# Block products in the output projection of a two-layer trunk, and where their sums are made

## The reference

```python
h = _rmsnorm(x, a_norm); proj = h @ a_w_in          # layer 0: conv, gated recurrence, SiLU gate
x = x + (y * silu(gate)) @ a_w_out                  # x1, 512 tokens by 2048
k, v = split(_rmsnorm(x, kv_norm) @ w_kv)           # 16 heads of 128
q, gate = split(_rmsnorm(x, b_norm) @ b_w_in)       # layer 1
o = stick_breaking_attention(q, k, v)
x = x + (o * silu(gate)) @ b_w_out                  # the output projection: 512 x 2048 by 2048 x 2048
return _rmsnorm(x, final_norm)
```

## Time and profile before

| | us |
|---|---|
| three runs: median, lowest, highest | 1676.51, 1676.43, 1677.09 |
| the profiled execution: its time | 1676.65 |
| the profiled execution: its span, first to last instruction | 1674.9 |
| PE, PEld, DVE, ACT, POOL busy | 1663.1, 1391.3, 1030.8, 818.3, 263.4 |
| one pair of heads in the attention stage (1170.66 to 1245.88) | 75.2 |
| last weight unit of attention issued, start of the score products behind it | 1476.87 |
| these score products issued | 1478.77 |
| last matmul issued | 1667.42 |

### The profile page before, as it was taken

How to read it: one execution, slowest core, us unless ns; L and a number is a source line. 1 busy time by engine, 2 the same in 40 slices (tenths; PEclk the granted TensorE clock), 3 DMA queues, 4 the chain that set the end, 5 groups by cost and what they waited for, 6 DMA issues and landing times.

```text
span 1674.9 us, 24069 instructions
## 1 busy us (share of the span) xinstructions
PE 1663.1 (99%) x7767; PEld 1391.3 (83%) x7767; DVE 1030.8 (62%) x1780; ACT 818.3 (49%) x1627; POOL 263.4 (16%) x251
## 2 busy tenths in 40 slices
PE   9999999999999999999999999999999999999998
PEld 7888888888888888887888888888888888888888
DVE  5788887778775554577655646465555646453333
ACT  7655566665555232355645545444444545432223
POOL 0121211122121222310002111101111111103100
PEclk9999999999999999999999999999999999999999
DMA  5555555665532333256755232323233232323223
GB/s 186 176 181 195 171 171 166 197 196 177 149 101 95 94 96 98 94 171 190 241 172 167 82 98 82 101 79 103 75 106 94 81 95 83 101 76 119 95 95 132
DMA packets 179606, 216.95 MB, mean 130 GB/s; under 512 B 12808, under 2 KB 137944, under 8 KB 179416
## 3 DMA queue, kind: packets, MB, share of 16 engines
q1 hardware_dynamic: 179544, 216.16, 41.3%
HBM read 190.95 MB, written 25.17 MB: 129 GB/s over the span
## 4 chain that ended last, share of the span: by engine, by line
PE 96%; DVE 1%; ACT 1%; SPq 1%; DMA 1%; issue 0%; POOL 0%; POOLq 0%; ACTq 0%; DVEq 0%
PE ps L549 94%; PE ps L731 1%; DMA rows_b<-in_b_norm 0%; PE ps L776 0%; SPq L401 0%; SPq L405 0%; SPq L382 0%; DMA v_stage<-in_w_kv 0%; PE ps L579 0%; DVE v_f L1440 0%; DVE rbuf L1335 0%; POOL y_lo L1652 0%; ACT w_hi L835 0%; PE ps L586 0%; DVE v_f L1432 0%
## 5 line engine op out<-in xcount | busy, mean ns | idle before, releaser
L549 PE MATMUL ps<-x_hi,w_hi 128*128 128x512 f32 x1408 | 551.0, 391 | 0.3 <-DVE x_lo L1232 0.3
L549 PE MATMUL ps<-x_hi,w_lo 128*128 128x512 f32 x1408 | 548.4, 389 | 0.0
L549 PE MATMUL ps<-x_lo,w_hi 128*128 128x512 f32 x1408 | 548.1, 389 | 0.0
L1196 DVE SCALAR_TENSOR_TENSOR w_lo<-stage,cT,w_hi 128x256 fp32r<-128x256 f32 x352 | 199.1, 566 | 328.7 <-ACT w_hi L839 328.1
L837 ACT ACTIVATE w_hi<-stage,cT 128x256 fp32r<-128x256 f32 x352 | 178.5, 507 | 375.5 <-PE ps L549 350.6
L549 PEld LDWEIGHTS ps<-x_hi,w_lo 128*128 128x128 f32 x1408 | 264.3, 188 | 55.2
L549 PEld LDWEIGHTS ps<-x_hi,w_hi 128*128 128x128 f32 x1408 | 264.4, 188 | 54.1 <-DVE x_lo L1232 0.5
L549 PEld LDWEIGHTS ps<-x_lo,w_hi 128*128 128x128 f32 x1408 | 264.5, 188 | 53.4 <-issue 0.2
L1193 DVE TENSOR_TENSOR w_lo<-stage,w_hi 128x512 fp32r<-128x512 f32 x160 | 132.6, 833 | 216.1 <-ACT w_hi L835 216.1
L835 ACT ACTIVATE w_hi<-stage 128x512 fp32r<-128x512 f32 x160 | 99.8, 630 | 251.2 <-PE ps L549 249.2
L839 ACT ACTIVATE w_hi<-stage,cT 128x256 fp32r<-128x256 f32 x352 | 174.4, 496 | 0.0
(11 more groups left out here) (206 smaller groups left out, 2301.5 us busy)
## 6 DMA issues: line engine op xcount, KB each, us to landing
stage<-in_a_w_in SPq DMA_DIRECT2D x160, 256.0 KB, 2.8
stage<-in_b_w_in SPq DMA_DIRECT2D x128, 256.0 KB, 2.8
stage<-in_w_kv SPq DMA_DIRECT2D x95, 256.0 KB, 2.8
stage<-in_a_w_out SPq DMA_DIRECT2D x80, 256.0 KB, 2.6
b_raw<-in_w_kv SPq DMA_DIRECT2D x64, 256.0 KB, 3.9
t_scratch<-b_raw SPq DMA_DIRECT2D x64, 256.0 KB, 3.5
stage<-in_b_w_out SPq DMA_DIRECT2D x64, 256.0 KB, 2.5
stage<-t_scratch SPq DMA_DIRECT2D x45, 256.0 KB, 3.1
```

The lines of the kernel that those rows point to most:

```text
L549: mm = pe.matmul(dst, a, b, start=start and n == 0, stop=stop and n == 2, skip_group_check=not check)
L1196: nc.vector.scalar_tensor_tensor(w_lo[:, slot, 0:256], stage[:, slot, 0:256], cT[:, col:col + 1], f(w_hi[:, slot, 0:256]), ALU.mult, ALU.s ...
```

## The change

**Seven products for eight.** O is seen as blocks: token halves (256) by even and odd heads, A11, A12, A21, A22; W as row tiles even and odd by column halves of 512 in each of two groups of 1024, B11, B12, B21, B22. PE makes p1 = A11 B11, p2 = A12 B21, p6, p7, p5 of block sums on both sides, p4 of A22 and a sum of B, p3 of a sum of A and B22, each over eight pairs of heads: 112 steps of six matmuls of 512 columns (`out_product`), two of them in the place of one unit of before while attention runs. Steps 0 to 55 are the first column group; p2, p4 and p3 come last, in turn. The weight ring has six slots. The first use of p7 and p5 stands ahead of the last of p6 (`out_operand`).

**Weight sums in the attention stage.** For each pair SP loads eight 256 KB blocks of W (`wb_load`, after pieces 14 and 18), DVE makes eight differences and sums (`weight_sum`, behind positions 2, 3, 4, 5, 8, 9, 14 and 15), SP stores them in `wt_scratch` (after pieces 22 and 33). In the output projection SP reads them back as operands.

**Sums of O on DVE.** Behind its gate products DVE makes the low part of A11, then three sums and, at position 31, the fourth (the semaphore `o_lo_ready`) and the low part of the second (`s2o_lo`). They go to `o_scratch` in DRAM (640 KB for a pair) and return to `or_raw`, which lies where x1 lay in SBUF, so the return waits for the end of the last weight unit of attention: seven pairs at step 10, the last at step 24. From there ACT and DVE split them in `or_hi` and `or_lo` inside their steps. POOL does none of this any more.

**x1 by tokens.** In stage 2 PE turns every x1 tile (`turn_x1`, eight calls of eight transposes, the last in the value stage), ACT copies it out, SP stores it; 4 MB come back into `x2` at step 24. The block results are added into `x2` by DVE.

**The end.** C11, C21 and C12 of the last column group become ready with the last three steps, for all four token tiles at once. DVE and ACT then add, square, multiply by the gain, norm, scale, first tiles 2 and 3, then 0 and 1.

The diff, cut to the parts of the output projection; indentation is cut too.

```diff
+OB_AT = {14 + 2 * i: i for i in range(VP)}
+OY_AT = {28 + 3 * i: i for i in range(VP)}
+W_SUM = {2: 0, 3: 1, 4: 2, 5: 3, 8: 4, 9: 5, 14: 6, 15: 7}
...
+def out_operand(q):
+    g, o = divmod(q, NO)
+    late = 2 * VP - 1
+    if late <= o < late + OUT_LAST:
+        return operand(q + 1)
+    if o == late + OUT_LAST:
+        return operand(g * NO + late)
+    return operand(q)
...
+def o_store(p, half):
...
+    sp.wait_ge(o_lo_ready, p * 2 + 3)
+    dst = o_scratch[at(p, 1), :, :].rearrange("n p c -> (n p) c")
+    sp.dma_start(dst, ost[:, half, 0:5, :].rearrange("p a c -> p (a c)")).then_inc(o_out, 16)
...
+def out_load(q):
...
+    if q >= VRING:
+        sp.wait_ge(po_lo, q - VRING + 1)
+    elif slot < RING:
+        sp.wait_ge(lo_ready, U4 - RING + slot + 1)
...
+for q in range(VOPS):
+    if q == 4:
+        sp.wait_ge(wb_out[0], 64 * VP)
+    out_load(q)
+    if q == 7:
+        wb_store(PAIRS - 1, 1)
+    if q == 10:
+        sp.wait_ge(w_used, U4)
+        sp.wait_ge(o_out, 32 + 16 * (PAIRS - 1))
+        for p in range(PAIRS - 1):
+            sp.dma_start(or_raw[:, p, :, :].rearrange("p a c -> p (a c)"),
+                         o_scratch[p]).then_inc(or_in, 16)
+    if q == 20:
+        o_store(PAIRS - 1, 1)
         g_row = final_norm.rearrange("(a n) -> a n", a=1)
+        sp.wait_ge(wb_out[1], 64 * VP)
         sp.dma_start(g_fin[:, :], g_row.to_broadcast([P, D])).then_inc(g_fin_in, 16)
+    if q == 24:
+        sp.wait_ge(s2o_lo, PAIRS)
+        x1_v = x1t_scratch.rearrange("(t p) n -> p t n", p=P)
+        for t in range(TT):
+            sp.dma_start(x2[:, t, :], x1_v[:, t, :]).then_inc(x1t_in, 16)
+        sp.wait_ge(o_out, 32 + 16 * PAIRS)
+        sp.dma_start(or_raw[:, PAIRS - 1, :, :].rearrange("p a c -> p (a c)"),
+                     o_scratch[PAIRS - 1]).then_inc(or_in, 16)
...
+def turn_x1(it, b, wait=None):
...
+    for m in range(2):
+        pe.wait_ge(res_step, it * 8 + (4 * b + m + 3))
+        if wait is not None:
+            pe.wait_ge(x1t_taken, wait)
+        for t in range(TT):
+            mm = pe.transpose(ps[2 + 4 * b + m][:, P * t:P * t + P], x1[:, m, P * t:P * t + P], ident[:, :])
+        mm.then_inc(x1_turned, 1)
...
+def out_product(q):
...
+    if name == "p6":
+        if g == 0:
+            pe.wait_ge(s2o_lo, i + 1)
...
+    if name in ("p7", "p5") and g == 0:
+        pe.wait_ge(ob_lo, i + 1)
+    if name in ("p2", "p4", "p3") and g == 0:
+        pe.wait_ge(oy_lo, i + 1)
...
+            if g:
+                pe.wait_ge(c12o_ready, 2 * g)
...
+            pe.wait_ge(c22o_ready, 2 * g + 2)
+    pe.wait_ge(po_lo, q + 1)
+    hi_w, lo_w = out_weights(q)
+    for t in range(2):
+        if name in O_LEFT:
+            m_hi, m_lo, which = O_LEFT[name]
...
+def out_step(q):
...
+        act.wait_ge(w_used, U4 - RING + q + 1)
+    elif q >= VRING:
+        act.wait_ge(po_used, q - VRING + 1)
+    nc.scalar.activation(out_weights(q)[0], out_staged(q), ACT.Copy).then_inc(po_hi, 1)
+    for at, parts, ready in ((OB_AT, slice(0, 2), ob_hi), (OY_AT, slice(2, 5), oy_hi)):
+        if q in at:
+            i = at[q]
+            act.wait_ge(or_in, 16 * (PAIRS - 1) if i < PAIRS - 1 else 16 * PAIRS)
+            if i >= 4:
+                act.wait_ge(s2o_lo, PAIRS)
...
+    if o == 2 * VP + AHEAD_V - 1:
+        act.wait_ge(po_used, OUT_OPERAND[g, VP - 1, "p6"] + 1)
+        if g == 0:
+            act.wait_ge(s2o_lo, PAIRS)
+        else:
+            act.wait_ge(u_added, 6 * g)
+            act.wait_ge(c12o_ready, 2 * g)
+            act.wait_ge(c21o_ready, 2 * g)
...
+def square(ready, g, t, first, c):
...
+    n = next(squared)
+    if n:
+        act.wait_ge(x2_sq, n)
+    nc.scalar.activation(junk[:, :], x2[:, t, 512 * c:512 * c + 512], ACT.Square,
+                         accum_out=ss5[:, t, c:c + 1]).then_inc(x2_sq, 1)
...
+def finish(n, t):
...
+    act.wait_ge(sqrt_in, 3 + n)
     nc.scalar.activation(small[:, 1, t:t + 1], small[:, 1, t:t + 1], ACT.Sqrt).then_inc(sqrt_out, 1)
-    act.wait_ge(rs_ready, 3 + t)
+    act.wait_ge(rs_ready, 3 + n)
+    act.wait_ge(gained, 4)
     nc.scalar.activation(x2[:, t, 0:D // 2], x2[:, t, 0:D // 2], ACT.Identity,
                          scale=rs_tok[:, t:t + 1]).then_inc(scaled_a, 1)
...
+def out_sums(it, half, pos):
...
+        dve.wait_ge(o_out, p * 16 + 16)
+        nc.vector.tensor_tensor(s1_o, a21, a22, ALU.add).then_inc(so_step, 1)
+        dve.wait_ge(so_step, p * 2 + 1)
+        nc.vector.tensor_tensor(s2_o, s1_o, a11, ALU.subtract).then_inc(s2o_raw, 1)
+        nc.vector.tensor_tensor(s3_o, a21, a11, ALU.subtract).then_inc(so_step, 1)
+    if pos == 31:
+        dve.wait_ge(s2o_raw, p + 1)
+        dve.wait_ge(so_step, p * 2 + 2)
+        dve.wait_ge(ost_copied, p + 1)
+        nc.vector.tensor_tensor(s4_o, s2_o, a12, ALU.subtract).then_inc(o_lo_ready, 1)
+        dve.wait_ge(s2o_hi, p + 1)
+        nc.vector.tensor_tensor(oa_lo[:, 0, one, :], s2_o, f(oa_hi[:, 0, one, :]),
+                                ALU.subtract).then_inc(s2o_lo, 1)
 def take_gate(it, half):
...
+def out_step(q):
...
+    hi_w, lo_w = out_weights(q)
+    dve.wait_ge(po_hi, q + 1)
+    nc.vector.tensor_tensor(lo_w, out_staged(q), f(hi_w), ALU.subtract).then_inc(po_lo, 1)
+    for at, parts, high, ready in ((OB_AT, slice(0, 2), ob_hi, ob_lo), (OY_AT, slice(2, 5), oy_hi, oy_lo)):
+        if q in at:
+            i = at[q]
+            dve.wait_ge(high, i + 1)
+            nc.vector.tensor_tensor(or_lo[:, i, parts, :], or_raw[:, i, parts, :],
+                                    f(or_hi(i)[:, parts, :]), ALU.subtract).then_inc(ready, 1)
+    g, o = divmod(q, NO)
...
+        dve.wait_ge(po_used, OUT_OPERAND[g, VP - 1, "p5"] + 1)
+        for t in (2, 3):
+            dve.wait_ge(p7o_added, 2 * g + t - 1)
+            piece(lambda x: nc.vector.tensor_tensor(x, x, ps[4 + t][:, :], ALU.subtract), g, t, 1,
+                  c22o_ready)
+    if g and o == AHEAD_V - 2:
+        make_c11(g - 1)
+    if g and o == AHEAD_V - 1:
+        make_c21(g - 1)
+    if g and o == AHEAD_V:
+        make_c12(g - 1, 0)
+        make_c12(g - 1, 1)
+    if g and o in GAIN_AT:
+        t, c = GAIN_AT[o]
+        if o == min(GAIN_AT):
+            dve.wait_ge(g_fin_in, 16)
+            dve.wait_ge(x2_sq, 8)
+        x = x2[:, t, 512 * c:512 * c + 512]
+        nc.vector.tensor_tensor(x, x, g_fin[:, 512 * c:512 * c + 512], ALU.mult)
+GAIN_AT = {2 * VP + 12 + 2 * n: (n % 4, n // 4) for n in range(8)}
+def piece(op, g, t, h, ready):
+    c = 1024 * g + 512 * h
+    op(x2[:, t, c:c + 512]).then_inc(ready, 1)
...
+    if g < VG - 1:
+        dve.wait_ge(po_used, OUT_OPERAND[g, VP - 1, "p3"] + 1)
+    else:
+        dve.wait_ge(last_done, t + 1)
+    dve.wait_ge(u_added, 6 * g + t + 5)
+    piece(lambda x: nc.vector.tensor_tensor(x, x, ps[6 + t][:, :], ALU.subtract), g, t, 1, c12o_ready)
...
+def gain(t, c):
+    x = x2[:, t, 512 * c:512 * c + 512]
+    nc.vector.tensor_tensor(x, x, g_fin[:, 512 * c:512 * c + 512], ALU.mult).then_inc(gained, 1)
+dve.wait_ge(x2_sq, 14)
+for t, c in ((2, 3), (3, 3), (2, 2), (3, 2)):
+    gain(t, c)
+def finish(n, t, squared):
     one = slice(t, t + 1)
-    link(nc.vector.tensor_reduce(ss[:, one], ss5[:, t, :], AX.X, ALU.add))
-    rsqrt(ss[:, one], small[:, 0, one], small[:, 1, one], small[:, 2, one], rs_tok[:, one], 3 + t,
-          lambda: take(ps[t], t, D - 256, 256))
-    dve.wait_ge(x2_taken, 4 * TT + t + 1)
-    nc.vector.tensor_scalar(x2[:, t, D // 2:D], x2[:, t, D // 2:D], rs_tok[:, one], None,
+    dve.wait_ge(x2_sq, squared)
+    link(nc.vector.tensor_reduce(ss[:, one], ss5[:, t, 0:4], AX.X, ALU.add))
+    rsqrt(ss[:, one], small[:, 0, one], small[:, 1, one], small[:, 2, one], rs_tok[:, one], 3 + n)
+for n, t in enumerate((2, 3)):
+    finish(n, t, 14)
+    if n == 0:
+        dve.wait_ge(gained, 4)
+    nc.vector.tensor_scalar(x2[:, t, D // 2:D], x2[:, t, D // 2:D], rs_tok[:, t:t + 1], None,
                             ALU.mult).then_inc(scaled_b, 1)
+for t in (0, 1):
+    gain(t, 2)
+make_c12(g, 0)
+make_c12(g, 1)
+for n, t in enumerate((0, 1)):
+    finish(2 + n, t, 15 + t)
+    dve.wait_ge(gained, 6)
+    nc.vector.tensor_scalar(x2[:, t, D // 2:D - 512], x2[:, t, D // 2:D - 512], rs_tok[:, t:t + 1], None,
+                            ALU.mult)
+    nc.vector.scalar_tensor_tensor(x2[:, t, D - 512:D], x2[:, t, D - 512:D], rs_tok[:, t:t + 1],
```

524 lines of the change are left out of this document (356 added, 168 removed).

## The result

The changed kernel takes 1696.88 us (median of 4 runs, 1695.06 to 1697.96), the kernel before 1676.61 in runs beside it: a ratio of 1.0119, 95% interval 1.0102 to 1.0137. It is slower, by 20.3 us; 1694.9 was predicted. Its profiled execution is the fastest of the four, 1695.06, with a span of 1693.3: 18.4 us longer than the span of before.

What follows compares the result with a forecast made beforehand. PE, busy 99% of a 1674.9 us span, was taken to bound the kernel. Terms: -24.3 + 14.9 + 4.9 + 6.5 + 12.4 + 3.8 = +18.2 us on 1676.65, so 1694.9; range 1680 to 1704.

Steps and rivals of the forecast that it cites:

- matmuls: Output projection on PE: matmuls removed against 112 x 6 added, transposes unchanged in number; -24.3 us, all on the path.
- end of the program: From last matmul to end: sums, squares, gains, norms, scalings and stores take 22.3 us instead of 7.4; +14.9, range +12 to +16.
- waits for DVE: Output projection: PE waits for DVE's sums, 2.1 and 1.3 first group, 1.3 second, 0.2 at its start; +4.9, bounds 2 and 9.
- first stretch: Stores, loads and seven returns, 6.4 MB, delay load 11: 4.5 us at step 11, 1.8 at value product, 0.2 later; +6.5.
- second stretch: From SP's wait at step 20, 7.87 MB including x1 delay step 25's load; +12.4 us, 3 of it at steps 21 and 22.
- clock: Two long PE waits halve TensorE's clock, one and a half steps at half speed each; +3.8 us, bounds 0 and 8.
- stages 2 to 4: x1 copies and stores, and attention's weight sums, cost nothing; bounds 0 and 2 for stages 2 and 3, -0.5 and 6 for 4.
- The large transfers hide: Rival: both stretches of large transfers cost nothing and the clock stays up; 1669.6 to 1672.2 us, faster; chance 0.12.
- Only the second stretch stalls: Rival: the first stretch is hidden, the second costs 11.9 us; sum +9.5, 1686 us; chance 0.15.
- more stalls: Rival: slow clock return, DRAM to SBUF at 350, late score products in attention; +5 to +14 on forecast, 1700 to 1709; chance 0.13.

Runs made afterwards that it cites:

- experiment 1: The changed kernel with its seven 640 KB returns split and spread over later steps, last weight-sum stores and g_fin's load moved later: 1687.1 us.
- experiment 2: The changed kernel with the 4 MB of x1 split into sixteen 256 KB pieces spread from step 21 on, g_fin loaded behind step 60: 1688.7 us.
- experiment 3: The changed kernel with x1 transferred twice behind step 24, the second time after the first has landed, 4.19 MB more: 1711.0 us.
- Experiment 4: The changed kernel with the edits of experiment 1 and experiment 2 together: 1683.9 us.
- experiment 9: The changed kernel with transfers spread further, SP's wait later, DVE's sums reordered, half the output finished early, a pair's last weight sum one position later: 1663.5 us.
- experiment 6: The changed kernel with the end reordered: C12 sums and squares first, one norm chain for all four tiles, norm and gain products merged: 1695.2 us.
- experiment 8: The changed kernel with DVE making the sums with p7 and C22 ahead of the low parts of steps 36 and 37: 1694.5 us.
- experiment 10: The kernel before plus 4.19 MB of idle transfers behind g_fin, ahead of output-projection load 15: 1677.1 us; with those transfers made twice: 1691.9 us.

## Why the prediction was right

1694.9 was predicted and 1695.06 is the time of the profiled execution, 1696.88 the median. The mechanism is right: two stretches of large transfers in SP's queue, the end and the sums of VectorE cost more than the saved matmuls. That the sum fits to 0.2 us is in part luck; where, is said below. The terms, from the profiled execution:

| | predicted | measured |
|---|---|---|
| matmuls | -24.3 | -24.3 (not measured by itself) |
| end of the program | +14.9 | +14.2 |
| waits for DVE | +4.9 | +5.1 |
| first stretch | +6.5 | +6.6 |
| second stretch | +12.4 | +12.1 |
| clock | +3.8 | +3.8 |
| small distances | | +0.9 |
| stages 2 to 4 | 0 | 0 |

**Matmuls and attention.** The score products of two pairs start 75.23 us apart (1106.97, 1182.20, 1257.43), as before (75.22), and no weight load waits from 900 to 1484 us: eight weight sums a pair cost nothing. The transposes moved; attention starts 6.2 us later, and I take as much off behind it, which no run measures by itself.

**First stretch.** Right in mechanism (experiment 1) and size, 3.7 + 2.9 against 4.5 + 1.8 + 0.2. The times of the text hold to about 1 us on an axis that is 6.2 later: the four stores left at 1486.56 (1480.4 + 6.2), load 11 landed at 1506.7 (1499.6 + 6.2, where the text's own terms add up to 1499.3) and PE began step 11 at 1508.3 (the operand: 1501.2 + 6.2). PE would have come at 1504.6 and not at 1502.9, mostly by the wait at step 1 that the text lacks. The rate of 390 GB/s held as a mean of unlike parts: the queue moved 198 and 261 GB/s in the windows 1490 to 1492 and 1492 to 1494 and 421 and 417 from 1495 to 1505; from the stores to the landing of load 11 it took 20.1 us in place of 19.2. What slowed its first part stays open.

**Second stretch.** Right in mechanism (experiments 2 and 3). The text had 3 us at steps 21 and 22 and 9.4 at 25; 3.2 and 8.9 were measured. Both ends of the wait came 2 us later than the text has them, even with the 6.2: SP was free at 1523.0 (1514.8 + 6.2) and PE began step 17 at 1523.4 (1515.2 + 6.2), and since PE's pace sets both, the difference kept. From 1526.5 to 1545.2 the queue moved 393 GB/s, the text's 390. Experiment 4 adds what the text gives only half: the time in which SP is held is queue time lost.

**Waits for DVE.** The sum is right and its parts are not. 2.1 and 1.3 at p4 and p3 were 1.6 and 1.2, 1.3 in the second group was 0.9, and 1.4 stood where the text has 0.2, at step 1. That one was missed: p6 goes into the banks in which the last gates lie, and DVE multiplies these only behind three low parts and a weight sum (it starts at 1486.45, PE was done with the gates at 1483.1). The wait is 0.6 shorter in experiment 9, where one weight sum stands behind these products.

**The clock.** It was halved twice, as taken, though the first time not by one wait: behind the 3.5 us before step 11 it stayed at 1.00, and it fell 0.8 us after PE had begun again behind the next wait. The term of one and a half steps was sized from no row; the trace has 3.4 and 4.3 us of work at half speed, of which half is lost. That this gives 3.8 is luck of the execution: the profiled one is the shortest of the four. The distances counted in experiment 3 lose 4.7 us in it, and 6.1 and 6.7 in the traces of experiments 6 and 8, whose kernels have the same two stretches. So other executions probably pay some 2 us more for the clock, which is also what the median has above the forecast; no trace shows those executions.

**The end.** With E = 1671.85 the steps came where the text has them: four gains done at E + 3.9 (4.0), C12 at E + 10.8 (11.1), tile 0 at E + 13.7 (14.0), tile 1 at E + 17.3 (17.6), the end at E + 21.5 (22.3). The text has the bound of this kernel right. What it does not have is the other bound behind it: it reads the end as a chain and never counts the output's bytes, and experiment 6 shows that with a shorter chain only 2.8 of the 14 us come back.

**The queue's rate.** The 5 us windows of the changed kernel with a share of 0.98 or more had 321, 384, 404, 417, 421 and 429 GB/s. As a limit of this core the 358 GB/s that the prediction cites from the Trainium skill are contradicted by five of these, and the Trainium skill itself says why: by DMA: Bandwidth & Descriptors, Measured (HBM→SBUF, 128 partitions, SWDGE, issued from GpSimd), that figure is a core's share while its neighbour streams too, and one core alone reached 425 GB/s with 16 MB. The highest windows of the trace agree with the 425. The Trainium skill's rule in that section, to batch DMAs to 1 MiB or more, is about the rate of one transfer; here pieces of 256 KB in place of 1 MB, with g_fin later (experiment 2), gave 8 us, since what counted was who stood behind them.

**The rivals.** "The large transfers hide" is out by experiments 3 and 10. "Only the second stretch stalls" is out by the wait of 3.5 us before step 11. Of "more stalls" the part in attention is out, which kept its 75.2; its slower clock was seen, in the longer executions.

## What to carry to other kernels

Saved matmuls are paid out only as far as what stood beside the old ones keeps pace: the steps take half as long, so that a slot of the ring covers half the time (four units of 2.72 us, 10.9, before; even with two slots more, six steps of 1.36, 8.2, now), and a burst that the kernel before could hide becomes a wait. Before putting a large transfer into a queue that feeds TensorE, divide its bytes by the queue's measured rate and compare with the time from the issue of the load behind it to TensorE's arrival at it (14.6 us in experiment 10, 8.7 before step 25); then break it into pieces, put them where the queue idles, and look for the place where the issuing engine itself waits. At the end of a program count the bytes still to be stored as well as the chain of small operations: finishing half of the output early, with one chain for the rest, took the end from 21.7 to 11.8 us, a shorter chain alone to 18.9.

## What was not expected of the hardware

Windows of 1 us in the changed kernel, around the wait before step 25 (last matmul before it at 1537.57, first behind it at 1546.70):

```profile
1539.00:1540.00 1.00, 0.00 (x0) 0.00 (x0) 0.00 (x0) 0.00 (x0) 0.00 (x0) 1.00 1.05 442
1540.00:1541.00 1.00, 0.00 (x0) 0.00 (x0) 0.00 (x0) 0.00 (x0) 0.00 (x0) 0.86 1.02 434
1541.00:1542.00 1.00, 0.00 (x0) 0.00 (x0) 0.00 (x0) 0.00 (x0) 0.00 (x0) 0.50 0.93 387
...
1550.00:1551.00 1.00, 1.00 (x4) 0.81 (x3) 1.00 (x3) 0.37 (x1) 0.00 (x0) 0.52 0.35 102
1551.00:1552.00 1.00, 1.00 (x6) 0.79 (x6) 1.00 (x2) 0.81 (x2) 0.00 (x0) 1.00 0.73 248
```

The granted clock goes from 2.4 to 1.2 GHz some 3.2 us after the last matmul's start and back 4.3 us after the first one's. The wait of 2.7 us before step 21 did not lower it (1.00 from 1530 to 1534), while the waits of 3.5 and 2.7 us before step 11 and the value product, with few matmuls between them, did, from 1513.4 to 1516.8.

The same wait does not always end in the same way. In the kernel of experiment 8, which is the changed kernel up to there, the wait before step 21 was 2.71 us again, and behind it the clock did fall, while PE was at work:

```profile
1533.00:1534.00 1.00, 1.00 (x5) 0.54 (x3) 1.00 (x2) 1.00 (x3) 0.00 (x0) 0.97 1.02 430
1534.00:1535.00 1.00, 0.81 (x3) 0.70 (x3) 1.00 (x3) 0.80 (x2) 0.00 (x0) 0.50 1.02 434
```

This is the likely reason why the runs of the changed kernel lie 2.9 us apart and those of the kernel before 0.7: their mean granted clocks are 0.991, 0.991, 0.990 and 0.989 for 1695.06, 1696.15, 1697.62 and 1697.96 us, where the kernel before has 0.999. By an estimate, 0.002 of the mean clock over 1695 us is 6.8 us more at half speed, of which work loses half, 3.4. What decides whether the clock falls behind such a wait stays open.
